# Gate modulation in the key pairs: four rounds of 512 columns in a row per pair, and rows turned by transposes

## The chip, the core and the metric

The kernel runs on one core of a Trainium2 chip. The metric is the device time of one execution in microseconds; lower is better. The engines are TensorE (PE; its weight loads are listed apart as PEld), VectorE (DVE), ScalarE (ACT), GpSimd (POOL) and SyncE (SP, which here only issues DMAs). Each has its own instruction stream; they meet only at semaphores.

## The reference

One layer of a hybrid decoder, for a prompt of 512 tokens and 8 sample sequences of 8 tokens (64), 576 token columns in all, with a model width D of 2048:

```python
mod = silu(c) @ w_ada + b_ada                     # 9 condition rows: 1 prompt, 8 samples
shift, scale, gate = split(mod, 3)                # 2048 columns each
h = rmsnorm(x, norm_pre) * (1 + scale) + shift
u = h @ w_in                                      # q, k, v, z, o, gates g_a, g_m ...
y_a = (attention(...) * silu(z_a)) @ w_br_a
y_m = (mlstm(...) * sigmoid(o) * silu(z_m)) @ w_br_m
y = (sigmoid(g_a) * y_a + sigmoid(g_m) * y_m) @ w_out
out = x + gate * rmsnorm(y, norm_post)
```

Shift and scale are needed before the first projection; gate is needed only at the very end.

## The kernel before

**Large products.** Weights come in granules of 256 KB into one of four slots of `w_raw` (SP's queue). ScalarE rounds a granule to `w_hi`, VectorE makes the remainder `w_lo` (`split_lo`), and TensorE multiplies three products: hi by hi, lo by hi, hi by lo. VectorE works three granules ahead of TensorE (`ahead`); `in_load` on SP waits on `lo_ready` until the slot's earlier granule is split, and ScalarE waits on `gemm_used` before it overwrites the slot's `w_hi`.

**First stage** (to about 187 us). 32 granules of the query columns, walked 2 row blocks at a time (`q_granule(n)`, j = n // 4, v = n % 4), because each row block of h is ready only when its shift and scale are. The shift and scale columns are made in 8 chunks: `ada_round(n)` multiplies a 1 MB piece of `w_ada` (`ada_in`, four buffers, loads of 512 KB on SP's queue, `ada_load`) by the condition rows padded to 32 columns (`c_pad`), 512 columns at a time, into `bank_a`, four matmuls side by side on four strips of the array (partitions 32t). Four rounds make a chunk. VectorE copies the bank to `mod_rows` (`ss_rows`), then `ada_rows` turns it to features: four plain fp32 matmuls with `pick`, a 128x9 matrix of ones and zeros that also sums the four strips, into 36 columns of `bank_o`; `ss_out` adds the bias in four small operations to `mod_ss`. POOL makes h from it (`s1`, `h_tmp`), ScalarE `h_hi`, VectorE `h_lo`. Between these, VectorE adds each granule's product into `q_acc` (`q_sum`), which frees the bank for the next one (`bank_free`).

**Pairs** (187 to 1134 us). Pairs of 128 columns, eight granules each: pairs 4 to 7 are the keys, 8 to 11 the attention values, and so on to 31. `k_or_v_pair` runs a key pair, with `to_tokens` (five transposes) after its first two granules for the pair before; `tok_k` on VectorE copies them and POOL stores them. In pairs 5 to 7 this is a loop (`Fori`). In pair 8 the gates of the mLSTM are summed in `bank_o` and `bank_a`. From pair 11 on, attention and mLSTM steps are laid between the granules. At 11 * NG + 4, `row_g`, `row_y` and `row_s` are turned to tokens by eleven small matmuls with the identity.

**Branch stage** (1134 to 1793 us). Four quads of 512 columns, each of 48 granules (`branch_quad(i)`, j = 0 .. 47): `ga` (16), `gm` (16), `ya` (8), `ym` (8). A granule is 12 matmuls of 512 columns and two for the samples. VectorE mixes at the end of `ya` and `ym` (`g_a`, `g_m`). Here the gate columns are made, 256 at a time in 8 chunks: after every sixth granule (j % 6 == 3) one `ada_g_round` of four matmuls of 256 columns on 9-column weights (`c_t`); the 512 KB pieces `ada_g` have one buffer and are loaded by POOL (`gate_in`), which waits on `ada_used` for each and stores and reloads `y_scratch` in between. VectorE copies four strips to `mod_row_g` at j = 22 and 46, TensorE turns them with two `pick` matmuls at j = 23 and 47, and `mod_out` adds the bias.

**Output stage** (to the end). Four quads of 16 granules with `w_out`. At kt == 9 of each, `gates_of(q)` spreads the gate over tokens with eight fp32 matmuls with the identity, four from `mod_g` broadcast and four from `g_exp`.

Of the kernel before, what the change touches and what calls it, by code (L numbers as in the profile page):

```python
# [66 lines left out]
ADA_N = ADA_CHUNKS * AQ  # L67

# [44 lines left out]
def build(nc, x_prompt, x_sample, cache_k, cache_v, state_C, state_n, state_m, page_table, c_prompt, c_sample,  # L113
# [11 lines left out]
    with ctx:  # L125
# [14 lines left out]
        def ada_slot(n):  # L140
            s = n % ADA_SLOTS
            return ada_late[s - 2] if s >= 2 and n >= ADA_N - 2 * AQ else ada_in[s]

# [34 lines left out]
        ada_late = [sb("ada_late0", "R1", 0, [P, AQ, AW]), sb("ada_late1", "R1", 4 * T, [P, AQ, AW])]  # L178
        v_att = sb("v_att", "R3", 0, [P, NT, DATT])
# [34 lines left out]
        c_t = sm("c_t", [P, KT, 9])  # L214
# [15 lines left out]
        pick = sm("pick", [P, 9])  # L230
# [107 lines left out]
        mod_row_g = sb("mod_row_g", "OT", 0, [P, CW])  # L338
        ada_g = sb("ada_g", "ROWS", 0, [P, AQ, CW])
# [29 lines left out]
        ada_g_ready = sem("ada_g_ready")  # L369
# [52 lines left out]
        def _(sp):  # L422
# [53 lines left out]
            p = 4  # L476
            for col, pairs in PH_PAIRS[1:]:
                with sp.Fori(max(p, 5), p + pairs) as i:
                    in_pair(i, sp.snap(col + (i - p) * CW))
                p += pairs  # L480
# [39 lines left out]
        def _(pe):  # L520
# [44 lines left out]
            def ada_rows(rows, n, blocks):  # L565
# [4 lines left out]
                for b in range(blocks):  # L570
                    done = mm(bank_o[:, 9 * b:9 * b + 9], rows[:, b * P:(b + 1) * P], pick[:])
# [86 lines left out]
            with pe.Fori(5, 8) as p:  # L658
                k_or_v_pair(p, 2 * (p - 5))

            for g in range(NG):
                in_granule(8, g)
                if g < 2:
                    to_tokens(stage[:, g, :], (bank_free[g], V0 + 8), (tok_done, 6 + g), tok_ps)
                if g == 4:
                    pe.wait_ge(gate_vec, 4)
# [48 lines left out]
            for x in range(11 * NG, 16 * NG):  # L715
# [14 lines left out]
                if x == 11 * NG + 4:  # L730
                    pe.wait_ge(rows_exp, 1)
                    pe.wait_ge(tok_done, 14)
                    for i in range(NT + 1):
                        n = P if i < NT else NS
                        mm(bank_s[0:n, 1, 4 * i:4 * i + 4], row_g[:, i * P:i * P + n], ident[0:HM, 0:HM])
                        mm(bank_s[0:n, 1, 32 + 4 * i:36 + 4 * i], row_y[:, i * P:i * P + n], ident[0:HM, 0:HM])
                    mm(bank_s[0:NB, 1, 64:68], row_s[:, 3 * NS:3 * NS + NB], ident[0:HM, 0:HM]).then_inc(rows_tok_ps, 1)
# [307 lines left out]
            def branch_quad(i):  # L1045
                for j in range(FGRAN):
# [14 lines left out]
            pe.wait_ge(pad_ready, 2)  # L1061
# [423 lines left out]
        def _(dve):  # L1485
# [24 lines left out]
            V.tensor_scalar(c_t[:].rearrange("p k c -> p (k c)"), c_th[:], 0.5, None, ALU.mult)  # L1510
# [14 lines left out]
            def mod_out(dst, blk, blocks, p, of):  # L1525

                dve.wait_ge(row_tp, p + 1)
                for b in range(blocks):
                    done = V.tensor_scalar(dst[:, blk + b, :], bank_o[:, 9 * b:9 * b + 9], vec_t[:, bass.ds(of + blk + b, 1)], None, ALU.add)
                done.then_inc(mod_done, 1)  # L1530
# [97 lines left out]
            for g in range(NG):  # L1628
# [22 lines left out]
                if g == 4:  # L1651
                    dve.wait_ge(gate_act, 2)
                    V.tensor_tensor(lf[:], lf2[:], lf[:], ALU.subtract).then_inc(gate_vec, 1)
            for cb in range(2):
# [10 lines left out]
            k_pair(5)  # L1665
            with dve.Fori(6, 8) as p:
# [13 lines left out]
            for g in range(NG):  # L1680
                ahead(8, g)
                if g in (1, 2):
# [261 lines left out]
            V.memset(mod_row_g[:], 0.0).then_inc(pad_ready, 1)  # L1944
# [80 lines left out]
            for x in range(S_F, S_END):  # L2025
# [17 lines left out]
                if kind == "out" and i == 0:  # L2043
                    if 3 <= kt < 7:
                        y_lo(12 + kt - 3)
                    if kt == 2:
                        mod_out(mod_g, 4 * (FQ - 1) + 2, 2, ADA_CHUNKS + 2 * FQ - 1, V_ADA + 2 * KT)
# [355 lines left out]
```

## Time and profile before

| | |
|---|---|
| median of 3 runs | 2010.16 us (2010.01 to 2010.32) |
| profiled execution, its own time | 2013.64 us |
| profiled execution, span of the profile | 2012.1 us |
| TensorE matmuls busy | 1966.6 us, 98% |
| VectorE, ScalarE, POOL busy | 784.6, 644.3, 212.5 us |
| bytes moved by DMA | 240.49 MB, mean 120 GB/s |

Busy time of TensorE counts matmuls from start to modelled end, and consecutive matmuls overlap; what a matmul adds to the time is therefore read from the starts of its neighbours. A row of the timeline gives the start, the length, engine, line, operation, destination and sources. A line such as L522 is a helper, used by all matmuls, so tiles tell the operations apart. A plain fp32 matmul leaves two records, a transpose one.

### The profile page before, as it was taken

Reading aid. Unit: us, or ns where it says so; the run is one execution under the profiler, and the core shown is the slowest. Engines: PE = TensorE matmul, PEld = TensorE weight load, DVE = VectorE, ACT = ScalarE, POOL = GpSimd, SP = SyncE. Lnnn points to the kernel's source line nnn. Section 1 sums busy time; section 2 is a strip of 40 time slices with the busy share of each in tenths; the row PEclk is TensorE's granted clock in tenths of the full one; section 3 lists DMA queues with packets and bytes.
Section 4 is the critical chain, followed back from the end, with each engine's and each line's share of the span. In section 5 each row is a group of like instructions: output and inputs, shape, how many; then the busy total and the mean of one; then the engine's idle time right before and its main releaser. Section 6 shows DMA issues by size and latency. Waiting matters only on the chain.

```text
span 2012.1 us, 31825 instructions
## 1 busy us (share of the span) xinstructions
PE 1966.6 (98%) x12466; PEld 1675.5 (83%) x12466; DVE 784.6 (39%) x1671; ACT 644.3 (32%) x1160; POOL 212.5 (11%) x351
## 2 busy tenths in 40 slices
PE   5999999999999999999999999999999999999997
PEld 4878999988899888888999877777777777778885
DVE  4555334256633234544444322422322232352224
ACT  4222222245445444432333222222212212332332
POOL 2220002000020101222410000000000000100001
PEclk9999999999999999999999999999999999999999
DMA  9983332231244532223532333343333343452223
GB/s 305 318 276 97 97 101 81 74 98 52 58 146 149 159 110 71 73 83 95 149 103 79 91 103 107 104 128 100 110 120 108 100 133 100 143 197 92 79 79 115
DMA packets 161841, 240.49 MB, mean 120 GB/s; under 512 B 15065, under 2 KB 113497, under 8 KB 159977
## 3 DMA queue, kind: packets, MB, share of 16 engines
q1 hardware_dynamic: 141600, 177.25, 29.3%
q0 software_dynamic: 17872, 61.28, 9.3%
q8 instruction: 89, 1.46, 0.3%
q10 hardware_dynamic: 2242, 0.19, 0.1%
q14 instruction: 38, 0.31, 0.0%
HBM read 220.93 MB, written 17.73 MB: 119 GB/s over the span
## 4 chain that ended last, share of the span: by engine, by line
PE 74%; DVE 1%; POOL 1%; issue 1%; ACT 1%; DMA 0%; ACTq 0%; POOLq 0%
PE gemm L522 58%; PE bank_s L522 8%; PE bank_o L522 3%; PE bank_a L522 3%; PE bank_s L754 1%; DVE g_m L1990 1%; PE bank_a L700 0%; PE bank_s L921 0%; PE bank_s L1042 0%; POOL hm_sq L2299 0%; POOL hm_sq L2300 0%; POOL rinv L2370 0%; ACT hm_sq L1124 0%; DVE y_tok L2082 0%; ACT w_hi L1124 0%
## 5 line engine op out<-in xcount | busy, mean ns | idle before, releaser
L1493 DVE TENSOR_TENSOR w_lo<-w_raw,w_hi 128x512 fp32r<-128x512 f32 x512 | 357.2, 699 | 808.0 <-ACT w_hi L1124 807.4
L522 PE MATMUL gemm<-h_hi,w_hi 128*128 128x288 f32 (+1 forms) x2560 | 666.4, 326 | 5.9 <-DVE q_acc L1563 2.4
L1124 ACT ACTIVATE w_hi<-w_raw 128x512 fp32r<-128x512 f32 x512 | 322.3, 630 | 1054.4 <-PE bank_s L522 590.7
L522 PE MATMUL gemm<-h_hi,w_lo 128*128 128x288 f32 (+1 forms) x2560 | 640.5, 316 | 0.0
L522 PE MATMUL gemm<-h_lo,w_hi 128*128 128x288 f32 (+1 forms) x2560 | 639.5, 315 | 0.0
L522 PEld LDWEIGHTS gemm<-h_hi,w_hi 128*128 128x128 f32 x2560 | 426.6, 189 | 86.2 <-issue 52.6
L522 PEld LDWEIGHTS gemm<-h_hi,w_lo 128*128 128x128 f32 x2560 | 427.3, 189 | 20.6
L522 PEld LDWEIGHTS gemm<-h_lo,w_hi 128*128 128x128 f32 x2560 | 426.9, 189 | 19.8
L522 PE MATMUL gemm<-w_hi,y_all 128*128 128x512 f32 x512 | 159.0, 392 | 0.4 <-DVE g_m L1990 0.4
L522 PEld LDWEIGHTS gemm<-w_hi,y_all 128*128 128x128 f32 x512 | 95.5, 188 | 25.2 <-DVE g_m L1990 1.1
L522 PE MATMUL gemm<-w_lo,y_all 128*128 128x512 f32 x256 | 99.9, 390 | 0.0
L2343 POOL DMA_DIRECT2D ada_g<-in_w_ada x32 | 24.1, 753 | 617.3 <-PE bank_a L522 481.5
L522 PE MATMUL gemm<-brm,w_hi 128*128 128x512 f32 x256 | 80.4, 395 | 0.0
L522 PE MATMUL gemm<-bra,w_hi 128*128 128x512 f32 x256 | 79.5, 392 | 0.0
L522 PEld LDWEIGHTS gemm<-bra,w_hi 128*128 128x128 f32 x256 | 47.8, 188 | 13.5 <-issue 1.7
L522 PEld LDWEIGHTS gemm<-brm,w_hi 128*128 128x128 f32 x256 | 47.1, 188 | 14.1 <-issue 3.4
L522 PEld LDWEIGHTS gemm<-w_lo,y_all 128*128 128x128 f32 x256 | 48.1, 188 | 10.2
L1756 DVE CUSTOM_DVE_ANT_0 e_map<-bank_s,alibi 128x128 f32<-128x128 f32 (+3 forms) x64 | 31.4, 491 | 56.9 <-PE bank_s L522 55.4
L522 PE MATMUL bank_s<-w_lo,h_smp 128*64 128x512 f32 x128 | 50.8, 397 | 0.0
L1124 ACT ACTIVATE e_map<-e_map,nmx 128x128 f32<-128x128 f32 (+3 forms) x64 | 35.5, 556 | 46.3 <-DVE nmx L1758 46.3
L522 PE MATMUL gemm<-brm,w_lo 128*128 128x512 f32 x128 | 49.9, 390 | 0.0
L522 PE MATMUL gemm<-bra,w_lo 128*128 128x512 f32 x128 | 49.9, 390 | 0.0
(454 smaller groups left out, 1794.7 us busy)
## 6 DMA issues: line engine op xcount, KB each, us to landing
w_raw<-in_w_in SPq DMA_DIRECT2D x384, 256.0 KB, 2.8
ada_in<-in_w_ada SPq DMA_DIRECT2D x56, 512.0 KB, 8.6
ada_g<-in_w_ada POOLq DMA_DIRECT2D x32, 512.0 KB, 4.3
w_raw<-in_w_out SPq DMA_DIRECT2D x64, 256.0 KB, 2.7
k_page<-in_cache_k POOLq DMA_DIRECT2D x16, 512.0 KB, 5.4
v_page<-in_cache_v POOLq DMA_DIRECT2D x16, 512.0 KB, 4.8
w_raw<-in_w_br_a SPq DMA_DIRECT2D x32, 256.0 KB, 2.7
w_raw<-in_w_br_m SPq DMA_DIRECT2D x32, 256.0 KB, 2.8
```

The costliest lines, as they stand in the source:

```text
L522: return nc.tensor.matmul(out, lhsT, rhs, start=start, stop=stop, skip_group_check=True)
L754: done = nc.tensor.transpose(bank_s[:, j // 2, (j % 2 * PAGES + pg) * P:(j % 2 * PAGES + pg + 1) * P], k_page[:, pg, h * P:(h + 1) * P], i ...
L1124: return nc.scalar.activation(out, in_, func, **kw)
L1493: V.tensor_tensor(w_lo[:, slot], w_raw[:, slot], w_hi[:, slot], ALU.subtract).then_inc(lo_ready, 1)
L1756: link(V.tensor_tensor_reduce(e_map[:, s % 2, c, 0:n], bank_s[:, c, 0:n], alibi[:, TP - n:TP], 1.0, LOW, ALU.add, ALU.max, mx[:, s % 2, c: ...
L1990: ins = V.scalar_tensor_tensor(g, g, 1.0, gemm[:, b // 2, b % 2, :], ALU.add, ALU.mult)
L2343: pool.dma_start(ada_g[:], w_ada2[r * AQ * P:(r + 1) * AQ * P, col:col + CW] .rearrange("(t p) c -> p t c", p=P)).then_inc(ada_g_ready, 16)
```

## The change

Gate columns are now made in pairs 4 to 7, 512 at a time in four chunks, by the same `ada_round` as shift and scale: after granule 6 of pair 4 + i, `gate_group(i)` runs the chunk's four rounds in a row. `ada_rows` follows after granule 0 of the next pair. The pieces are loaded by SP (`gate_load`), two DMAs of 512 KB each with whole 512-column rows, into the two `ada_in` buffers in R4 and two new ones in R3, at places in SP's order given by `GATE_LOADS`. The rounds, row copies, `mod_out` and `gate_in` of the branch stage go, as do `c_t`, `pick`, `ada_g`, `mod_row_g`. `ada_rows` uses four 128x128 transposes, so the four strips are no longer summed there: `ss_out` and `gate_out` sum them by `tensor_reduce` and then add the bias. The eleven matmuls of the row turn and the eight of `gates_of` become transposes. The loops over pairs 5 to 7 are written out.

```diff
+GATE_CHUNKS = 4
+GATE_LOADS = {NG * (5 + i) + at: (ADA_CHUNKS + 1 + i) * AQ + r for i in range(GATE_CHUNKS - 1) for r, at in enumerate((5, 6, 8, 10))}
+GATE_LOADS.update({NG * 4 + 7: ADA_N + 2, NG * 5: ADA_N + 3})
...
+        ada_gate = [ada_in[0], ada_in[1], sb("ada_gate2", "R3", 0, [P, AQ, AW]), sb("ada_gate3", "R3", AQ * AW, [P, AQ, AW])]
...
+            def gate_load(n):
+                i, r = n // AQ - ADA_CHUNKS, n % AQ
+                sp.wait_ge(ada_used, n - ADA_SLOTS + 1)
+                if n == ADA_N + 2:
+                    for cb in range(2):
+                        sp.wait_ge(bank_free[cb], V0 + 4)
+                col = 2 * D + i * AW
+                for half in range(2):
+                    row = (AQ * r + 2 * half) * P
+                    sp.dma_start(ada_slot(n)[:, 2 * half:2 * half + 2, :], w_ada2[row:row + 2 * P, col:col + AW]
+                                 .rearrange("(t p) c -> p t c", p=P)).then_inc(ada_ready[n % ADA_SLOTS], 16)
...
+                if n in (QN - 5, QN - 3):
+                    gate_load(ADA_N + (n - QN + 5) // 2)
             in_load(4, NG - 1, COL_KA)
+            gate_load(GATE_LOADS[5 * NG - 1])
...
+                    in_load(p, g, col)
+                    if NG * p + g in GATE_LOADS:
+                        gate_load(GATE_LOADS[NG * p + g])
...
                 for b in range(blocks):
-                    done = mm(bank_o[:, 9 * b:9 * b + 9], rows[:, b * P:(b + 1) * P], pick[:])
+                    done = nc.tensor.transpose(bank_o[:, b * P:(b + 1) * P], rows[:, b * P:(b + 1) * P], ident[:])
...
+            def gate_group(i):
+                for r in range(AQ):
+                    ada_round(ADA_N + AQ * i + r)
+
             def k_or_v_pair(p, n):
 
                 for g in range(NG):
                     in_granule(p, g)
+                    if g == 0 and p > 4:
+                        ada_rows(mod_rows, ADA_CHUNKS + p - 5, AQ)
+                    if g == 6:
+                        gate_group(p - 4)
...
-                        mm(bank_s[0:n, 1, 4 * i:4 * i + 4], row_g[:, i * P:i * P + n], ident[0:HM, 0:HM])
+                        nc.tensor.transpose(bank_s[0:n, 1, 4 * i:4 * i + 4], row_g[:, i * P:i * P + n], ident[0:HM, 0:HM])
...
-            def ada_g_round(i, r):
-
-                if r == 0:
-                    pe.wait_ge(row_out, ADA_CHUNKS + i)
-                pe.wait_ge(ada_g_ready, 16 * (AQ * i + r + 1))
-                for t in range(AQ):
-                    done = mm(bank_a[32 * t:32 * t + 9, 0:CW], c_t[:, AQ * r + t, :], ada_g[:, t, :], start=r == 0, stop=r == AQ - 1)
-                done.then_inc(ada_used, 1)
...
-                    if j % 6 == 3:
-                        ada_g_round(2 * i + j // 24, j // 6 % 4)
-                    if j in (23, 47):
-                        ada_rows(mod_row_g, ADA_CHUNKS + 2 * i + j // 24, 2)
...
-                    mm(bank_o[:, b * P:(b + 1) * P], mod_g[:, 4 * q + b, 0:1].to_broadcast([P, P]), ident[:])
+                    nc.tensor.transpose(bank_o[:, b * P:(b + 1) * P], mod_g[:, 4 * q + b, 0:1].to_broadcast([P, P]), ident[:])
                 for b in range(4):
-                    done = mm(bank_a[0:NS, b * P:(b + 1) * P], g_exp[:, b, :], ident[:])
+                    done = nc.tensor.transpose(bank_a[0:NS, b * P:(b + 1) * P], g_exp[:, b, :], ident[:])
...
+            def quarters(b, blocks):
+                return bank_o[:, b * P:(b + blocks) * P].rearrange("p (b t x) -> p b x t", t=AQ, x=32)[:, :, 0:9, :]
+
+            def gate_out(i):
+
+                dve.wait_ge(row_tp, ADA_CHUNKS + i + 1)
+                out = mod_g[:, AQ * i:AQ * i + AQ, :]
+                of = V_ADA + 2 * KT + AQ * i
+                link(V.tensor_reduce(out, quarters(0, AQ), AX.X, ALU.add))
+                V.tensor_tensor(out, out, bcast(vec_t[:, of:of + AQ], 9), ALU.add).then_inc(mod_done, 1)
...
-                for b in range(AQ):
-                    blk = b // 2 * KT + 2 * c + b % 2
-                    done = V.tensor_scalar(mod_ss[:, blk, :], bank_o[:, 9 * b:9 * b + 9], vec_t[:, V_ADA + blk:V_ADA + blk + 1], None, ALU.add)
+                for part in range(2):
+                    blk = part * KT + 2 * c
+                    link(V.tensor_reduce(mod_ss[:, blk:blk + 2, :], quarters(2 * part, 2), AX.X, ALU.add))
+                for part in range(2):
+                    blk = part * KT + 2 * c
+                    done = V.tensor_tensor(mod_ss[:, blk:blk + 2, :], mod_ss[:, blk:blk + 2, :], bcast(vec_t[:, V_ADA + blk:V_ADA + blk + 2], 9), ALU.add)
                 done.then_inc(mod_done, 1)
...
             def k_pair(p):
                 for g in range(NG):
                     ahead(p, g)
+                    if g == 1:
+                        gate_out(p - 5)
                     if g in (1, 2):
                         tok_k(2 * (p - 5) + g - 1)
+                ss_rows(ADA_CHUNKS + p - 4)
...
-            for n in range(2 * FQ * AQ - 2):
-                gate_in(n // AQ, n % AQ)
-                if n % (2 * AQ) == 0 and n:
-                    y_store(n // (2 * AQ) - 1)
+            for i in range(FQ - 1):
+                y_store(i)
```

## Rows read from the trace of the kernel before

**Rows 1.** Busy time by stretch: PE, PEld, DVE, ACT, POOL, PEclk, DMA share, GB/s.

```profile
40.00:172.00 132.00, 129.62 (x1000) 104.24 (x997) 68.73 (x124) 31.08 (x50) 27.57 (x56) 0.99 0.84 267
...
187.00:330.00 143.00, 143.00 (x1074) 140.71 (x1074) 52.70 (x119) 34.16 (x56) 14.80 (x19) 1.00 0.34 93
...
1134.00:1793.00 659.00, 657.57 (x3074) 511.24 (x3073) 205.72 (x346) 161.00 (x266) 36.27 (x55) 1.00 0.36 113
```

**Rows 2.** Chain of waits: start, length, what; an input pair, a branch granule.

```profile
561.53 3.19 PE gemm L522 x24
...
1197.38 2.73 PE gemm L522 x12
```

**Rows 3.** Waits of TensorE, 1120 to 1830 and 30 to 172: total, times, longest.

```profile
PEld gemm L522 <- DVE g_m L1990: 4.3, 8, 0.8
...
PE gemm L522 <- DVE q_acc L1563: 2.4, 6, 0.4
```

**Rows 4.** Timeline of TensorE around a gate round in the branch stage.

```profile
1206.57 0.40 PE L522 MATMUL bank_s<-w_lo,h_smp 128*64 128x512 f32 x1
1206.89 0.62 PE L522 MATMUL bank_a<-ada_g,c_t 128*9 128x256 f32 x8
1207.44 0.50 PE L522 MATMUL gemm<-h_hi,w_hi 128*128 128x512 f32 x1
1207.78 0.40 PE L522 MATMUL gemm<-h_lo,w_hi 128*128 128x512 f32 x1
```

**Rows 5.** Timeline of TensorE around the row turn at j = 23.

```profile
1213.71 0.40 PE L522 MATMUL bank_s<-w_lo,h_smp 128*64 128x512 f32 x1
1213.95 0.51 PE L522 MATMUL bank_o<-pick,mod_row_g 128*128 128x9 f32 x4
...
1214.62 0.39 PE L522 MATMUL gemm<-h_lo,w_hi 128*128 128x512 f32 x1
```

**Rows 6.** Timeline of TensorE around the four transposes of `fold_features`.

```profile
1193.35 0.39 PE L522 MATMUL bank_s<-w_lo,h_smp 128*64 128x512 f32 x1
1193.58 0.60 PE L1042 MATMUL bank_s<-ident,s_copy 128*128 128x128 f32 x4
...
1194.24 0.39 PE L522 MATMUL gemm<-h_lo,w_hi 128*128 128x512 f32 x1
```

**Rows 7.** Timeline of TensorE around `gates_of` (the row at 1819.22 is left out).

```profile
1816.98 0.40 PE L522 MATMUL bank_s<-w_lo,y_all 128*64 128x512 f32 x1
1817.21 1.06 PE L522 MATMUL bank_o<-ident,mod_g 128*128 128x128 f32 x8
...
1819.78 0.40 PE L522 MATMUL gemm<-w_lo,y_all 128*128 128x512 f32 x1
```

**Rows 8.** Instructions that read `row_g`: duration min/median/max, first and last start.

```profile
L522 PE MATMUL bank_s<-ident,row_g x10: 194/248/268, 393.8 to 395.8; 4*128 4x4 f32 x8, 4*64 4x4 f32 x2
```

**Rows 9.** Timeline of TensorE around the row turn in the first stage.

```profile
68.36 0.43 PE L522 MATMUL gemm<-h_hi,w_lo 128*128 128x288 f32 x2
68.64 0.95 PE L522 MATMUL bank_o<-pick,mod_rows 128*128 128x9 f32 x8
...
69.79 0.42 PE L522 MATMUL gemm<-h_lo,w_hi 128*128 128x288 f32 x2
```

**Rows 10.** VectorE: `ss_out` in the timeline, and the reductions of `lam_s`.

```profile
69.63 0.63 DVE L1546 TENSOR_SCALAR mod_ss<-bank_o,vec_t 128x9 f32<-128x9 f32 x4 [1.86 <-PE bank_o L522]
...
L1643 DVE TENSOR_REDUCE lam_s<-lam_p x2: 220/220/220, 189.0 to 189.5; 128x1 f32<-128x64 f32 x2
```

**Rows 11.** Timeline of TensorE around four rounds in the first stage.

```profile
63.01 0.43 PE L522 MATMUL gemm<-h_hi,w_lo 128*128 128x288 f32 x2
63.37 3.64 PE L522 MATMUL bank_a<-ada_in,c_pad 128*32 128x512 f32 x32
...
67.31 0.42 PE L522 MATMUL gemm<-h_lo,w_hi 128*128 128x288 f32 x2
```

**Rows 12.** DMAs into `ada_in`: time from issue to landing.

```profile
DMA to landing us min/median/max: 3.6/8.6/18.3
```

More of the change, by code:

```diff
@@ L141, in ada_slot @@
             s = n % ADA_SLOTS
+            if n >= ADA_N:
+                return ada_gate[s]
             return ada_late[s - 2] if s >= 2 and n >= ADA_N - 2 * AQ else ada_in[s]
@@ L337, in build @@
         assert work[0] == 5632
-        mod_row_g = sb("mod_row_g", "OT", 0, [P, CW])
-        ada_g = sb("ada_g", "ROWS", 0, [P, AQ, CW])
         g_exp = sb("g_exp", "OT", 0, [P, 4, NS])
@@ L474, in in_pair @@
                     in_load(p, g, col)
-            p = 4
-            for col, pairs in PH_PAIRS[1:]:
-                with sp.Fori(max(p, 5), p + pairs) as i:
+            for p, col in [(p, COL_KA + (p - 4) * CW) for p in (5, 6, 7)] + [(8, COL_VA)]:
+                for g in range(NG):
+                    in_load(p, g, col)
+                    if NG * p + g in GATE_LOADS:
+                        gate_load(GATE_LOADS[NG * p + g])
+            p = 8
+            for col, pairs in PH_PAIRS[2:]:
+                with sp.Fori(max(p, 9), p + pairs) as i:
                     in_pair(i, sp.snap(col + (i - p) * CW))
@@ L657, in _ @@
             pe.wait_ge(x_out_a, 2 * (NT + 1))
-            with pe.Fori(5, 8) as p:
+            for p in range(5, 8):
                 k_or_v_pair(p, 2 * (p - 5))
@@ L664, in _ @@
                     to_tokens(stage[:, g, :], (bank_free[g], V0 + 8), (tok_done, 6 + g), tok_ps)
+                if g == 0:
+                    ada_rows(mod_rows, ADA_CHUNKS + 3, AQ)
                 if g == 4:
+                    pe.wait_ge(mod_done, ADA_CHUNKS + GATE_CHUNKS)
                     pe.wait_ge(gate_vec, 4)
@@ L734, in _ @@
                         n = P if i < NT else NS
-                        mm(bank_s[0:n, 1, 4 * i:4 * i + 4], row_g[:, i * P:i * P + n], ident[0:HM, 0:HM])
-                        mm(bank_s[0:n, 1, 32 + 4 * i:36 + 4 * i], row_y[:, i * P:i * P + n], ident[0:HM, 0:HM])
-                    mm(bank_s[0:NB, 1, 64:68], row_s[:, 3 * NS:3 * NS + NB], ident[0:HM, 0:HM]).then_inc(rows_tok_ps, 1)
+                        nc.tensor.transpose(bank_s[0:n, 1, 4 * i:4 * i + 4], row_g[:, i * P:i * P + n], ident[0:HM, 0:HM])
+                        nc.tensor.transpose(bank_s[0:n, 1, 32 + 4 * i:36 + 4 * i], row_y[:, i * P:i * P + n], ident[0:HM, 0:HM])
+                    nc.tensor.transpose(bank_s[0:NB, 1, 64:68], row_s[:, 3 * NS:3 * NS + NB], ident[0:HM, 0:HM]).then_inc(rows_tok_ps, 1)
                     pe.wait_ge(rows_tok, 1)
@@ L1523, in row_copy @@
                 V.tensor_copy(dst, src).then_inc(row_out, 1)
[L1525 to L1530, printed above, removed]
+            def quarters(b, blocks):
[6 more added lines that the diff above has]
+                V.tensor_tensor(out, out, bcast(vec_t[:, of:of + AQ], 9), ALU.add).then_inc(mod_done, 1)
             def x_out(tt):
@@ L1659, in k_pair @@
                     ahead(p, g)
+                    if g == 1:
+                        gate_out(p - 5)
                     if g in (1, 2):
                         tok_k(2 * (p - 5) + g - 1)
+                ss_rows(ADA_CHUNKS + p - 4)
                 for cb in range(2):
                     keep(p, cb, 2 * (p - 4) + cb)
-            k_pair(5)
-            with dve.Fori(6, 8) as p:
+            for p in range(5, 8):
                 k_pair(p)
@@ L1681, in _ @@
                 ahead(8, g)
+                if g == 1:
+                    gate_out(3)
                 if g in (1, 2):
@@ L2046, in _ @@
                     if kt == 2:
-                        mod_out(mod_g, 4 * (FQ - 1) + 2, 2, ADA_CHUNKS + 2 * FQ - 1, V_ADA + 2 * KT)
-                        dve.wait_ge(mod_done, ADA_CHUNKS + 8)
+                        dve.wait_ge(mod_done, ADA_CHUNKS + GATE_CHUNKS)
                         link(V.tensor_tensor(mod_g[:], mod_g[:], bcast(vec_t[:, V_POST:V_POST + KT], 9), ALU.mult))
@@ L2056, in _ @@
                     mix(kind, m)
-                if x < S_G:
-                    j = x - S_F - FGRAN * i
-                    if j in (22, 46):
-                        dve.wait_ge(ada_used, ADA_N + AQ * (2 * i + j // 24 + 1))
-                        for t in range(AQ):
-                            done = V.tensor_copy(mod_row_g[32 * t:32 * t + 9, :], bank_a[32 * t:32 * t + 9, 0:CW])
-                        done.then_inc(row_out, 1)
-                    if j == 26:
-                        mod_out(mod_g, 4 * i, 2, ADA_CHUNKS + 2 * i, V_ADA + 2 * KT)
-                    if j == 2 and i:
-                        mod_out(mod_g, 4 * i - 2, 2, ADA_CHUNKS + 2 * i - 1, V_ADA + 2 * KT)
                 if kind == "out" and kt == n - 1 and i < FQ - 1:
@@ L2119, in _ @@
                                  pattern=[[1, P]], channel_multiplier=-1))
-            for t in range(AQ):
-                link(G.affine_select(out=pick[:], in_=pick[:], compare_op=ALU.not_equal, fill=1.0, base=-32 * t,
-                                     pattern=[[-1, 9]], channel_multiplier=1))
             link(G.memset(g_pick[:], 0.0))
@@ L2335, in _ @@
                 pool.dma_start(n_sample[0, :, hd, :], n_out[:]).then_inc(n_outs, 16)
[L2338 to L2344 removed]
             pool.wait_ge(c_outs[1], 64 * HM)
[L2347 to L2350 removed]
+            for i in range(FQ - 1):
+                y_store(i)
             pool.wait_ge(y_stored, 64 * (FQ - 1))
             pool.wait_ge(gemm_used, S_F + FGRAN * (FQ - 1) + 2 * KT)
[L2353 to L2359 removed]
+            for blk in range(12):
                 y_load(blk)
```

22 lines of the change are left out of this document (1 added, 21 removed).

## The prediction, made before the changed kernel was run

> **What bounds the kernel now.** I read the stretches first. In all three shown, TensorE is busy for nearly the whole stretch at a granted clock of 0.99 to 1.00 (2.4 GHz), while VectorE, ScalarE and the DMA engines have room [rows 1]. The chain of waits says the same in detail: it is made of matmuls back to back, 24 of 288 columns in 3.19 us (0.266 us a pair) in the input pairs, and 12 of 512 columns in 2.73 us (0.2275 us each) in the branch stage [rows 2]. So whatever TensorE executes inside a stretch lengthens it by its own start-to-start time, and whatever is taken out gives that time back. The waits show the few places where this is not so: in the branch stage TensorE waits 4.3 us for VectorE's `g_m` (the mixing at the end of `ym`, eight times), and in the first stage 2.4 us, six times, for `q_acc` [rows 3]. Work removed just before such a wait gives nothing.
>
> **What is removed from the branch stage.** There are 32 `ada_g_round` calls (4 quads times `j % 6 == 3`, 8 each). Around one, the last ordinary matmul starts at 1206.57 and the second ordinary one after the round at 1207.78: 1.21 us, of which two ordinary steps are 0.455, so a round costs 0.755 [rows 4]. 32 x 0.755 = 24.2 us. At the borders ga to gm and ya to ym a round stands before a new bank; I count these in full, because no wait for ScalarE is recorded at gm to ya, which has no round there either.
>
> The eight `ada_rows(mod_row_g, ..)` calls: from 1213.71 to 1214.62, again two ordinary steps plus the call, 0.91 - 0.455 = 0.455 [rows 5]. Four of them (j = 23) give it back: 1.8 us. The four at j = 47 stand right before the wait for `g_m`, which VectorE ends by its own order; TensorE will come 0.455 earlier and wait 0.455 longer. I put these at nothing. Bounds for the eight: 1.8 to 3.6. VectorE's 32 row copies and its `mod_out` work, and POOL's 32 loads and their waits, go too; neither is on the path.
>
> **What becomes a transpose.** `fold_features` does four 128x128 transposes: from 1193.35 to 1194.24, 0.89 - 0.455 = 0.435 us, 0.11 each [rows 6]. `gates_of` does eight fp32 matmuls of 128 columns: from 1816.98 to 1819.78 with three ordinary steps, 2.80 - 0.68 = 2.12 us, 0.265 each [rows 7]. As transposes 8 x 0.11 = 0.87, so 1.25 saved, four times: 5.0 us. The Trainium skill ("TensorE: Matmul & The Clock Gate", section Terms) calls the transpose mode four times faster for fp32; by that, `gates_of` would take 0.53 and the four calls would give 6.4. Rows 6 and 7 show 2.4 times, and the sum goes by them.
>
> The turn of `row_g` and `row_y`: five of each and one of `row_s` in turn, in two passes each, starting from 393.8 to 395.8 [rows 8], with the last one some 2.2 us. Eleven at 0.11 are 1.2, so 1.0 is saved. The wait for `rows_tok` behind it stays. Bounds: 0.5 (if tiny transposes have an issue cost of their own) to 1.5.
>
> **The first stage.** The eight `ada_rows` there have four matmuls: from 68.36 to 69.79, 1.43 - 0.53 = 0.90 us [rows 9]; as transposes 0.435, so 0.465 less on TensorE. But right behind it VectorE runs `ss_out`, a `w_lo` and the `q_acc` sum that frees the bank for which TensorE then waits. `ss_out` is four operations in 0.63 us now [rows 10] and becomes two reductions of 72 elements, each waited for, and two additions. The nearest row is a reduction of 64 elements at 220 ns [rows 10]; two of them start at 189.0 and 189.5 with a multiplication of 64 elements between, each waited for, so 0.26 for each waited operation at most. 2 x 0.26, and 0.37 for the two additions (an estimate: 0.16 for each of the four operations now, a little more for 18 elements): 0.89, which is 0.26 more. VectorE starts 0.35 to 0.45 earlier and runs 0.26 longer: six chunks give 0.1 each rather than 0.465. The chunk without `q_acc` sums gives 0.47 in full; the first `ss_out`, which starts late because of the three `w_lo` before it, costs 0.26 before the first matmul. Sum 0.8 us saved. Bounds: reductions twice as dear (+0.44 each call) lose 6 x 0.34 + 0.7 - 0.5 = 2.2; all transposes given back gives 3.3.
>
> **What is added to pairs 4 to 7.** `gate_group(i)` is four `ada_round` calls in a row, 16 matmuls of 512 columns on 32-column weights, four side by side. The first stage has just this group: from 63.01 to 67.31, 4.30 - 0.53 = 3.77 us, 0.94 a round [rows 11]. A round of 512 columns thus costs 0.94 against 2 x 0.755 for the two of 256 that it replaces. 4 x 3.77 = 15.1 us. Four `ada_rows` of four transposes at 0.435: 1.7 us. Both lie on the path, since TensorE is 143.00 of 143.00 us busy there [rows 1]. VectorE gets per pair one row copy (0.7 us) and one `gate_out` (0.5), in a stretch in which it is busy 52.7 of 143 us and works three granules ahead, some 9 us: hidden. Behind `gate_out` stand `tok_k` and the next `w_lo`; both have more than a granule.
>
> **The moved loads.** 16.8 MB go from POOL's queue to SP's, 32 DMAs of 512 KB. SP sends the `w_raw` load of a granule when the split of the granule four earlier is done, some seven granules ahead of TensorE; ScalarE can use it once TensorE is three granules ahead, so a load has four granules less the split, some 11 us, of cover. `gate_load` waits for a used slot: for group i+1 the first two are let go by the rounds of group i itself, the last is queued behind the `w_raw` load of granule 10 (the next pair's third), which goes when TensorE has ended the pair's granule 2 and the split has followed, 1.3 us later. Its round comes after granule 6 and three rounds: 4 x 3.19 + 2.8 - 1.3 = 14.3 us. A 512 KB load in the crowded first stage landed in 8.6 us at the median and 18.3 at the longest [rows 12], where the core moved 267 GB/s. In the pairs it moves 93 [rows 1], and 16.8 MB over some 120 us add 140: 233 GB/s, below what the first stage reached. I cost the wait at nothing. The first group has even more time (its last two loads wait for the `q_acc` tiles in R3 to be read, six granules before use). `h_hi` and `h_lo` tiles are no longer touched. Without this cover each late microsecond counts once per pair.
>
> **The sum.** Saved: 24.2 + 1.8 + 5.0 + 1.0 + 0.8 = 32.8. Added: 15.1 + 1.7 = 16.8. Net 16.0 us less. The profiled execution spans 2012.1 us (2013.6 with what lies around it), 3.5 above the median of the runs; I take the difference as unchanged: span 1996.1, median 2010.2 - 16.0 = 1994.2.
>
> **The rivals.**
> *The groups wait for their loads (slower).* Place: TensorE before the fourth round of groups 1 to 3, SP's queue behind it. Up to a landing time of 14.3 us nothing happens; at 18.3, the longest seen, three waits of 4.0, 12 us: 2006. It decides the sign when three waits take 16.0, that is at 19.6 us; at 23 they take 26 and the time is about 2020. For it: 512 KB loads and 256 KB `w_raw` loads share one queue, and a blocked SP holds back both. Against: the measured rate has room. 5 in 100 for slower, 7 in 100 for a partial wait (1997 to 2006).
> *VectorE decides the first stage.* `ss_out` with dear reductions, and the h chain (POOL, ScalarE, VectorE) behind it late by the same: 2 to 5 us lost, 1997 to 2001. For it: six waits for `q_acc` now. 12 in 100.
> *More comes back than I count.* Faster transposes, the j = 47 calls counted, the first stage giving all: 1.8 + 2.5 + 1.4 + 0.5, at most 6: 1988 to 1991. 10 in 100.
> *The branch rounds were no cost.* If the removed rounds filled time in which TensorE had to wait for the split weights, the time would rise by 15.1 + 1.7 - 6.8 = 10 us, 2020. Against it, ScalarE is busy 161 and VectorE 206 of the 659 us there [rows 1]. 1 in 100.
> *The clock falls behind runs of transposes.* There are 17 places with new ones; a granule of 3.19 us at 1.2 GHz behind each would cost 54 us, 2048. The input pairs already hold `to_tokens` transposes twice a pair and run at 1.00 [rows 1]. 2 in 100. The Trainium skill (the same page, Part 4) says that transposes do not count as TensorE being busy in the way that matmuls do; by that rule this case would be real only if a run of them were long, and here it is below 1 us.
> *My sum:* 63 in 100, 1991 to 1997.
>
> **Range and chances.** From 1989.5 to 2002.0: it leaves out the slow rivals (8 in 100), half of the partial wait and some of the gains. Faster by over 0.2% (4 us, about what a measurement of this kernel can tell from no change): all cases that end below 2006, 0.91. Within it 0.03, slower 0.06.
>
> **What would show each step.** In the profile after: no matmul of `ada_g`, and branch granules one after the other; stretch 1134 to 1793 shorter by 26 us. Groups of 16 matmuls in pairs 4 to 7, each 3.6 to 3.8 us with no idle time before it; if TensorE shows waits for DMAs of `ada_in` or `ada_gate` there, the first rival is true. `gates_of` 0.9 us. VectorE's `mod_ss` group 0.8 to 1.0 us, and TensorE's wait for `q_acc` near 0.4 us as before; above 0.7 us the second rival. TensorE's wait for `g_m` grows by about 1.8 us. The pairs 4 to 8 become 16.8 us longer. The prediction is wrong if the groups cost well over 3.8 us, for which a wait or a lower clock must be seen.

## The result, and the profile after

| | before | after |
|---|---|---|
| median | 2010.09 us (2009.66 to 2010.32) | 1992.62 us (1992.08 to 1994.67) |
| profiled execution: span of the profile | 2012.1 us | 1990.6 us |
| TensorE matmuls busy | 1966.6 us | 1940.9 us |

The ratio is 0.991, with a 95% interval of 0.9898 to 0.9923: 17.5 us less, where 16.0 had been forecast. Both kernels were run once more: after 1992.65 us against 2010.71 for before beside it, and before unchanged 2010.65 against 2011.21. The medians of before, in all sets of executions, run from 2010.1 to 2011.2 us, so a median moves by some 0.5 to 1 us. Single executions moved by up to 2.6 us for the kernel after (4 and 4 executions) and by up to 6.4 for before (2009.24 to 2015.6 among 15).

The stretches of the profile after, with the columns of [rows 1]:

```profile
40.00:172.00 132.00, 127.01 (x980) 101.12 (x972) 70.19 (x125) 31.06 (x50) 27.66 (x56) 0.99 0.84 267
187.00:330.00 143.00, 143.00 (x1090) 129.56 (x1091) 42.74 (x89) 29.95 (x49) 10.67 (x16) 1.00 0.59 189
1134.00:1793.00 659.00, 656.73 (x2932) 528.98 (x2931) 201.77 (x321) 169.42 (x279) 15.58 (x29) 1.00 0.31 98
```

In the pairs TensorE is still busy for all of 143.00 us, with DMA traffic twice that of [rows 1] (189 against 93 GB/s). Now the waits of TensorE that answer to [rows 3], the whole execution's list (total, times, longest):

```profile
PEld gemm L543 <- DVE g_m L2018: 5.6, 8, 0.8
...
PE gemm L543 <- DVE q_acc L1587: 4.0, 6, 0.7
...
PE gemm L543 <- DVE g_m L2018: 2.2, 8, 0.4
...
PE bank_o L947 <- DMA n<-in_state_n: 1.6, 1, 1.6
```

For 187 to 330 us the same view lists no wait of TensorE at all: the groups of rounds never waited for a load. The wait for `g_m` grew from 4.3 to 5.6 on the weight loads, and from 1.4 to 2.2 on the matmuls. These are two views of the same pauses (two at the end of each quad), so they are not added; the 4.3 of [rows 3] is the weight loads' figure. The wait for `q_acc` grew from 2.4 to 4.0.

The timeline of the kernel after at a group of rounds in pair 4, at the row turn (rows 410.11 to 410.55, alike, left out), at `gates_of`, and at `ss_out` in the first stage:

```profile
209.34 0.42 PE L543 MATMUL gemm<-h_hi,w_lo 128*128 128x288 f32 x2
209.70 1.93 PE L543 MATMUL bank_a<-ada_in,c_pad 128*32 128x512 f32 x16
211.44 1.90 PE L543 MATMUL bank_a<-ada_gate,c_pad 128*32 128x512 f32 x16
213.27 0.53 PE L543 MATMUL gemm<-h_hi,w_hi 128*128 128x288 f32 x2
213.64 0.42 PE L543 MATMUL gemm<-h_lo,w_hi 128*128 128x288 f32 x2
...
410.03 0.22 PE L767 MATMUL bank_s<-ident,row_g 4*128 4x4 f32 x1
...
410.61 0.16 PE L769 MATMUL bank_s<-ident,row_s 4*8 4x4 f32 x1
411.31 0.53 PE L543 MATMUL gemm<-h_hi,w_hi 128*128 128x288 f32 x2 [0.54 <-DVE dec_tok L1772]
...
1800.43 0.40 PE L543 MATMUL bank_s<-w_lo,y_all 128*64 128x512 f32 x1
1800.66 0.60 PE L1089 MATMUL bank_o<-ident,mod_g 128*128 128x128 f32 x4
1801.10 0.60 PE L1091 MATMUL bank_a<-ident,g_exp 128*64 128x128 f32 x4
...
1802.01 0.39 PE L543 MATMUL gemm<-w_lo,y_all 128*128 128x512 f32 x1
...
87.87 0.60 PE L592 MATMUL bank_o<-ident,mod_rows 128*128 128x128 f32 x4
...
88.51 0.50 DVE L1567 TENSOR_REDUCE mod_ss<-bank_o 128x18 f32<-128x72 f32 x2 [1.50 <-PE bank_o L592]
...
89.04 0.27 DVE L1570 TENSOR_TENSOR mod_ss<-mod_ss,vec_t 128x18 f32<-128x18 f32 x2
...
90.72 0.50 PE L543 MATMUL gemm<-h_hi,w_hi 128*128 128x288 f32 x2 [0.66 <-DVE q_acc L1587]
```

A group is 16 + 16 records, with no idle time before any of them. From 209.34 to 213.64, less two ordinary steps (0.53), it takes 3.77 us, just what [rows 11] gave. The row turn starts at 410.03 and its eleventh transpose at 410.61: 0.6 us, where [rows 8] had some 2.2. `gates_of` is 1802.01 - 1800.43 less three ordinary steps (0.68): 0.90 us, where [rows 7] had 2.12. `ss_out` is two reductions in 0.50 and two additions in 0.27.

**Where the time went.** Starts of the same instructions, read from the tile views, cut the span into parts. The two right columns use the second profile of before and of after; the first profile of before lay above its median, and the part in bold is why.

| part of the span, us | before | after | before again | after again | forecast change |
|---|---|---|---|---|---|
| start to the row turn | 393.8 | 410.0 | 393.2 | 409.0 | +16.0 |
| row turn to the first `exp` of `e_map` | 9.4 | 6.2 | 9.3 | 6.2 | -1.0 |
| first `z_act` to the head step's `c_a` transposes | **135.1** | 132.3 | 132.3 | 133.9 | 0 |
| last `z_act` to the last `s_copy` (branch stage) | 657.9 | 631.3 | 658.0 | 631.3 | -26.0 |
| last `s_copy` to the end | 220.5 | 215.5 | 220.5 | 215.5 | -5.0 |

The parts not shown are the same to 0.2 us. Between the second profiles the span falls from 2008.6 to 1991.3: 15.8 - 3.1 + 1.6 - 26.7 - 5.0 = -17.4. Three rows are as forecast to within 0.7 us; the row turn gives three times its term; and the part in bold, which the change does not touch, differs from one execution to the next. So does the first part, by up to 1.0 us between two profiles of one kernel (410.0 and 409.0).

### The profile page after: what moved, and what is told of

Same layout as the page of the kernel before. It is cut to its first block, busy times and chain, and to the rows that moved or that the text cites. A ratio compares the mean times of both kernels' runs of the same rounds, so it can differ in the third digit from the quotient of the medians.

```text
span 1990.6 us, 31173 instructions
## 1 busy us (share of the span) xinstructions
PE 1940.9 (98%) x12247; PEld 1661.4 (83%) x12247; DVE 773.6 (39%) x1633; ACT 644.4 (32%) x1160; POOL 187.7 (9%) x314
## 4 chain that ended last, share of the span: by engine, by line
PE 74%; DVE 1%; POOL 1%; issue 1%; ACT 1%; DMA 0%; ACTq 0%; POOLq 0%
PE gemm L543 58%; PE bank_s L543 9%; PE bank_o L543 3%; PE bank_a L543 2%; PE bank_s L786 1%; DVE g_m L2018 1%; PE bank_a L732 0%; PE bank_s L953 0%; PE bank_s L1065 0%; POOL hm_sq L2311 0%; POOL hm_sq L2312 0%; POOL rinv L2366 0%; ACT hm_sq L1142 0%; DVE y_tok L2098 0%; PE bank_s L572 0%
## 5 line engine op out<-in xcount | busy, mean ns | idle before, releaser
L543 PEld LDWEIGHTS gemm<-h_hi,w_lo 128*128 128x128 f32 x2560 | 425.4, 188 | 20.3
L2292 POOL DMA_DIRECT2D y_scratch<-g_a x12 | 6.5, 546 | 574.9 <-DVE g_a L2037 574.1
```

What stands on the lines that cost most here:

```text
L543: return nc.tensor.matmul(out, lhsT, rhs, start=start, stop=stop, skip_group_check=True)
L2292: pool.dma_start(y_scratch[4 * i + b], g_a[:, b, :]).then_inc(y_stored, 16)
```

## The experiments

**The first two: both kernels again.** The kernels after and before, unchanged, beside others.

> The changed kernel unaltered, beside the others on one chip. My sum: 16 us below the kernel before. The theory that the granted clock adds to it (it stood at 0.68 for 5 us behind the row turn and at 0.50 for 5 us behind the head-3 mLSTM step in the profile before, and at 1.00 in both places in the one after): 17 to 18 us below, because the fall behind the row turn is gone in every run (1.4 us), while the fall behind the head-3 step comes and goes and spreads single times over some 3 us.

Measured: 1992.65 us (1991.78 to 1993.91), ratio 0.9909 (0.9894 to 0.9924). It is 18.1 below the 2010.71 beside it, nearer to the 17 to 18 of the clock theory than to the 16 of the sum, but the first set gave 17.5, so the medians alone hardly decide between the two.

The later experiments are given against this 1992.65, though some were run in other sets. The kernel before had 2010.71 in this set (with the row turn by matmuls, the transposes alone, and after without gate work), 2010.56 beside rounds apart, late loads, `pick` and the small vector first, and 2010.27 beside the last three; differences across sets are uncertain by about as much.

> The kernel before, unaltered, for a second profile of it. The first was taken of an execution 3.5 us above the median. From the start of the row turn to the first attention exponential it took 9.4 us there (9.3 in e1, 6.2 wherever the turn is made of transposes), and from the first z_act to the sample states' transposes 135.1 us (132.2 to 133.9 in the others). If the fall of the clock behind the row turn belongs to the matmul turn, the first interval is again 9.3 to 9.4, and the second, which comes and goes, is 132 to 134. If both come and go, the first can be near 7.8.

Measured: 2010.65 us, ratio 0.9997 (0.9988 to 1.0006), span 2008.6 us. The earlier profiled execution of before, at 2012.1, was thus no picture of its median: the bold 135.1 above is 132.3 in this one.

**The row turn by matmuls in the kernel after.**

```diff
-  nc.tensor.transpose(bank_s[0:n, 1, 4 * i:4 * i + 4], row_g[..], ident[0:HM, 0:HM])
+  mm(bank_s[0:n, 1, 4 * i:4 * i + 4], row_g[..], ident[0:HM, 0:HM])
   (the same for row_y and row_s)
```

> The changed kernel with the eleven transposes of the row turn put back to matmuls with the identity. My sum's term: 1.0 us more than e0; by the start times of the two profiles 1.6 (2.2 us against 0.6). If the clock theory holds, the turn takes 1.6 us more and the granule behind it shows a granted clock well below 1.00 again, which costs another 1.4: 3.0 more in all.

Measured: 1995.25 us, ratio 0.9923 (0.9909 to 0.9936): 2.6 above the kernel after beside it, where the term was 1.0. Windows around the turn tell why; the columns are those of [rows 1], and the granted clock is the third number from the end. First this kernel:

```profile
409.30:412.20 2.90, 2.36 (x24) 2.22 (x23) 0.51 (x6) 0.63 (x1) 0.00 (x0) 1.00 0.24 82
412.20:417.50 5.30, 5.30 (x29) 4.90 (x29) 0.96 (x2) 0.28 (x1) 1.90 (x4) 0.68 0.19 49
```

The kernel before, and before again:

```profile
396.70:402.00 5.30, 5.24 (x28) 4.88 (x28) 1.03 (x3) 0.28 (x1) 1.89 (x4) 0.68 0.18 49
```

```profile
397.00:402.00 5.00, 5.00 (x28) 4.72 (x27) 0.75 (x4) 0.63 (x1) 1.15 (x3) 0.68 0.18 52
```

The kernel after:

```profile
410.00:411.30 1.30, 0.77 (x12) 0.64 (x11) 0.49 (x6) 0.63 (x1) 0.00 (x0) 1.00 0.50 165
411.30:415.00 3.70, 3.69 (x28) 3.52 (x28) 0.99 (x2) 0.14 (x1) 1.90 (x4) 1.00 0.27 71
```

With matmuls, the 5 us behind the turn ran at a mean granted clock of 0.68, between the two levels of 2.4 and 1.2 GHz. With transposes they ran at 1.00, and the same 28 or 29 matmul records took 3.7 us in place of 5.3. So the turn gives twice: 1.6 us of its own, and about 1.5 of clock behind it. The interval from the turn to `e_map` was 9.3 to 9.4 us in all four profiles with the matmul turn (before twice, this one, and the kernel before without gate work) and 6.1 to 6.2 in the ten others.

**The transposes alone, in the kernel before** (row turn and `gates_of`; the first stage as it was).

> The kernel before with only the row turn and the eight matmuls of each gates_of made transposes; nothing moved. My sum: 5.0 + 1.0 = 6.0 us below before. With the clock theory 5.0 + 1.6 + 1.4 = 8.0 below. The rule that a transpose is four times faster than an fp32 matmul would give 6.4 + 1.6 = 8.0 without any change of clock; the start times in gates_of tell the two apart (0.9 us for eight, or 0.5).

Measured: 2004.56 us, ratio 0.9967 (0.9954 to 0.9981), 6.15 less than before. By its profile against before again: -3.1 at the turn, -5.0 in the output stage, but the part shown in bold was 133.8 and not 132.3, 1.5 more, and 0.6 more to the row turn; span 2002.7 against 2008.6. The median thus lies at the 6.0 of the sum and not at the 8.0 of the clock theory; the profile has the whole 8.1 of the two changed places and loses 2.1 elsewhere. The experiment on the head step below shows what the 1.5 of it is.

**The kernel after without gate work.**

```diff
-  if g == 6:
-      gate_group(p - 4)
   (and the gate row turns, row copies, gate_out, gate_load and their waits)
+  V.memset(mod_g[:], 1.0)
```

> The changed kernel without the gate part of the modulation: no gate loads, rounds, row copies, row transposes and gate_out; mod_g is filled with ones. My sum: 16.8 us below e0 (four groups of 3.77, four row turns of 0.43), with no other difference. If the added loads or VectorE work cost TensorE anything beyond their own matmuls, the gap is above 18; if part of the groups is hidden somewhere, it is below 15.

Measured: 1976.06 us, ratio 0.9824 (0.9809 to 0.9839): 16.6 below the kernel after. The added work costs what the sum said, 16.8, to within 0.2 by the medians and 0.4 by the profiles (the row turn starts at 392.6 in place of 409.0): next to nothing of it is hidden, and next to nothing is lost around it.

**The kernel before without gate work.**

```diff
-  if j % 6 == 3:
-      ada_g_round(2 * i + j // 24, j // 6 % 4)
-  if j in (23, 47):
-      ada_rows(mod_row_g, ADA_CHUNKS + 2 * i + j // 24, 2)
   (and the row copies, mod_out and gate_in)
+  V.memset(mod_g[:], 1.0)
```

> The kernel before without the gate part of the modulation: no rounds, row turns, copies and loads in the branch stage; mod_g is filled with ones. My sum for what the branch stage gives back: 26.0 us below before (32 rounds at 0.755, four row turns, four more hidden behind the wait for g_m). If rounds at the borders of products had been hidden, eight of 32, the gap is near 20; if all row turns count, 27.8. The two profiles give 26.6 for the stretch.

Measured: 1984.0 us, ratio 0.987 (0.9852 to 0.9887): 26.3 below before, 26.0 forecast. Its branch stage is 631.3 us, as in the kernel after.

**The rounds apart, one after each of granules 3 to 6 of the pair.**

```diff
-  if g == 6:
-      gate_group(p - 4)
+  if g >= 3 and g < 7:
+      ada_round(ADA_N + AQ * (p - 4) + g - 3)
```

> The changed kernel with the four rounds of a gate chunk laid apart, one after each of granules 3 to 6 of the pair instead of all after granule 6. If a run of four saves only the columns, no change. By the rows: a lone round of 256 columns cost 0.755, a round of 512 in a run of four 0.94; if a lone round has a fixed part for getting in and out of the four-strip matmuls (0.4 us if the column part of 256 is half of 0.85), a lone one of 512 costs about 1.15 to 1.2, so 16 x 0.2 to 0.25 = 3 to 4 us more than the changed kernel.

Measured: 1997.48 us, ratio 0.9933 (0.9919 to 0.9946), 4.8 above the kernel after. The timeline of a lone round:

```profile
231.33 0.42 PE L543 MATMUL gemm<-h_hi,w_lo 128*128 128x288 f32 x2
231.68 1.06 PE L543 MATMUL bank_a<-ada_in,c_pad 128*32 128x512 f32 x8
232.68 0.53 PE L543 MATMUL gemm<-h_hi,w_hi 128*128 128x288 f32 x2
233.04 0.42 PE L543 MATMUL gemm<-h_lo,w_hi 128*128 128x288 f32 x2
```

From 231.33 to 233.04 less two ordinary steps (0.53) is 1.18 us, against 0.94 in a run of four. Sixteen rounds at 0.24 more are 3.8 us; the period of a pair, from one `mod_rows` copy to the next, is 31.7 us in place of 30.9, which is 3.4 in all. That is most of the 4.8; the rest was not placed. A round costs its border as well as its columns, so putting four in a row is a part of the gain in its own right.

**The gate loads late in SP's order.**

```diff
-  for r, at in enumerate((5, 6, 8, 10))
+  for r, at in enumerate((7, 8, 10, 14))
```

> The changed kernel with the loads of groups 1 to 3 sent later: at positions 7, 8, 10, 14 of SP's order instead of 5, 6, 8, 10. The last piece then goes about 1.5 us before its round can start, instead of 14.3. In the profile after, pieces landed in 5.5 us (4.3 to 6.7). First rival's mechanism: three waits of 4 to 5 us each, 12 to 15 us more than the changed kernel, and TensorE's waits name the DMA into ada_gate. If the group hides the wait, or the clock falls behind it, the sum differs: a fall of the clock adds up to 3 us each.

Measured: 2013.95 us, ratio 1.0018 (1.0009 to 1.0027), 21.3 above the kernel after. The list of waits and the timeline at one of them:

```profile
PE bank_a L543 <- DMA ada_gate<-in_w_ada: 14.7, 3, 5.0
```

```profile
242.08 1.04 PE L543 MATMUL bank_a<-ada_gate,c_pad 128*32 128x512 f32 x8
247.99 1.93 PE L543 MATMUL bank_a<-ada_gate,c_pad 128*32 128x512 f32 x8 [4.87 <-DMA ada_gate<-in_w_ada]
249.85 0.85 PE L543 MATMUL gemm<-h_hi,w_hi 128*128 128x288 f32 x2
250.50 0.68 PE L543 MATMUL gemm<-h_lo,w_hi 128*128 128x288 f32 x2
250.98 0.68 PE L543 MATMUL gemm<-h_hi,w_lo 128*128 128x288 f32 x2
...
252.26 0.42 PE L543 MATMUL gemm<-h_hi,w_lo 128*128 128x288 f32 x2
```

The wait itself is 4.9 us, yet it costs about 6.9: the round behind it takes 1.86 us from start to start in place of 0.94, and the next pairs start 0.48 apart in place of 0.27, which is TensorE at 1.2 GHz until about 252. From one group to the next it is 37.8 and 37.7 us where the kernel after has 30.9, so the first two waits cost 6.9 and 6.8; from the third group to the row turn it is 6.6 more. Together that is 20.3, and the row turn starts 20 to 21 us later. The waits alone, 14.7, are what the first rival's mechanism was expected to give (12 to 15); the rest is what comes behind them. The first rival was a real danger: with loads sent two to four granules later in SP's order the whole gain is gone. In the kernel after the slack held, but it was smaller than the prediction's 14.3 us. Its last group has the last load issued and the third of its rounds started so:

```profile
293.43 0.99 SPq L449 DMA_DIRECT2D ada_gate<-in_w_ada  x2
```

```profile
304.02 1.90 PE L543 MATMUL bank_a<-ada_gate,c_pad 128*32 128x512 f32 x16
```

The second DMA is issued at 293.94 and the fourth round starts at 304.88: 10.9 us. In the two groups before it is 12.0 and 11.4. `ada_gate` landed in 5.5 us at the median and 6.7 at the longest, so some 4 us were left, not 8.

**The strips summed by `pick` again,** in the first stage and for the four gate turns; `ss_out` and `gate_out` four additions each, as before.

```diff
-  done = nc.tensor.transpose(bank_o[:, b * P:(b + 1) * P], rows[:, b * P:(b + 1) * P], ident[:])
+  done = mm(bank_o[:, 9 * b:9 * b + 9], rows[:, b * P:(b + 1) * P], pick[:])
```

> The changed kernel with the twelve row turns put back to fp32 matmuls with pick, and with the four small additions in place of reductions. My sum: 0.8 us back in the first stage, and four turns in the pairs at 0.90 instead of 0.43: 1.9. Together 2.7 us more than the changed kernel. The theory that VectorE eats the first stage's saving entirely: 1.9 us more or less than that; the theory that transposes pay in full: 12 x 0.465 = 5.6 more.

Measured: 1995.83 us, ratio 0.9923 (0.9909 to 0.9936), 3.2 above the kernel after, 2.7 forecast. Four gate turns at 0.465 are 1.9 of it, which leaves 1.3 for the first stage, for which the sum had 0.8. In the first stage of the kernel after, a chunk takes 18.71 us from one `mod_rows` copy to the next, and took 18.89 before: 0.18 saved, where the prediction had 0.1. Six such are 1.1.

**The sum that frees a bank first, then `ss_out`.** VectorE's order in the first stage, at v == 1:

```diff
-  if v == 1 and more:
-      ss_out(c + 1)
   early_lo(n + LOOKAHEAD)
-  if c:
-      q_sum(c, v, n)
+  if v == 1 and more:
+      if c:
+          q_sum(c, v, n, (0,))
+      ss_out(c + 1)
+      if c:
+          q_sum(c, v, n, (1,))
+  elif c:
+      q_sum(c, v, n)
```

> The changed kernel with one order changed on VectorE in the first stage: at v == 1 the split of the next granule and the q_acc sum of the first bank go before ss_out, not behind it. In the profile after, TensorE waits 0.66 us for that sum in six chunks, while VectorE stands idle 1.5 us before each ss_out. If this wait is what eats the saving of the row transposes there, it goes and the time falls by 4.0 us (6 x 0.66). If the later ss_out then holds up h (about 0.2 us later, with some 1 us of room), less: 1 to 3 us, with waits for h_lo or h_tmp in its place.

Measured: 1988.67 us, ratio 0.989 (0.9872 to 0.9907), 4.0 below the kernel after (3.5 if each is taken against before in its own set), as expected. A chunk takes 17.82 us, 0.89 less and not the 0.66 of the wait; this holds for five intervals, 4.5 us, and the interval before them is about 1 us longer (19.1, against 17.7 and 18.4 in the two profiles of the kernel after). So there is luck in how well the 4.0 came out. The list of waits of 30 to 180 us has no wait of TensorE for VectorE's `q_acc` any more, and instead:

```profile
PEld gemm L543 <- DVE h_lo L1576: 1.0, 1, 1.0
...
PE bank_s L543 <- POOL h_tmp L2198: 0.8, 1, 0.8
...
PE gemm L543 <- ACT q_acc L1142: 0.6, 1, 0.6
```

These are short and come once each; the h chain mostly has room for an `ss_out` that comes a little later. So the kernel after was held in each of six chunks by `ss_out` standing ahead of the `q_acc` sum: the place that the prediction's second rival named, though it cost a few us by the order of VectorE's work and not through a dear reduction. The kernel before has the same order and waits for `q_acc` six times too [rows 3]; the edit was not tried there.

**The small state vector loaded before the large state.** At the last mLSTM head TensorE waits 1.6 us for `n` (the fourth row of the waits above), whose DMA stands behind the four loads of the large state on POOL's queue.

```diff
+  pool.dma_start(n0[:], state_n[0]).then_inc(in_n0, 16)
   state_in(0, 0)
-  pool.dma_start(n0[:], state_n[0]).then_inc(in_n0, 16)
```

> The changed kernel with one order changed on POOL: the small load of the sample states n goes before the four loads of the states C, not behind them (2.9 us of issuing). In the profiles before and after TensorE waits 1.6 us for it, at the end of 6 us in which it is busy 4.5, and behind this the clock stood at 0.50 once and at 1.00 once. Wait alone: 1.6 us less. If the stretch is also what lets the clock fall, the single times also lie closer together and the median falls by 2 to 3 us.

Measured: 1990.39 us, ratio 0.9899 (0.9884 to 0.9915), 2.3 below the kernel after. The wait is gone from the list (its 1.6 us is most of the 2.3), and the part in bold of the table is 130.7 us here and 130.6 in the next kernel. In the others it was 132.1 to 132.3 in four profiles, 133.7 to 133.9 in seven and 135.1 in one. The windows of this place, at the same distance behind the first `z_act` to 0.1 us, in the first profile of before:

```profile
890.00:895.00 5.00, 4.67 (x19) 4.65 (x20) 4.26 (x15) 0.35 (x1) 0.81 (x2) 0.50 0.12 33
895.00:900.00 5.00, 5.00 (x34) 5.00 (x34) 0.76 (x2) 0.63 (x1) 0.00 (x0) 0.83 0.31 79
```

in before again:

```profile
889.20:894.20 5.00, 4.67 (x35) 4.66 (x36) 4.31 (x16) 0.98 (x2) 0.95 (x2) 1.00 0.13 33
```

and in the two profiles of the kernel after:

```profile
903.00:908.00 5.00, 4.71 (x35) 4.69 (x36) 4.34 (x16) 0.98 (x2) 0.87 (x2) 1.00 0.12 34
```

```profile
901.90:906.90 5.00, 4.61 (x23) 4.59 (x24) 4.25 (x15) 0.35 (x1) 0.87 (x2) 0.66 0.11 31
```

One and the same kernel ran this stretch at 0.50 in one execution and at 1.00 in another: 19 matmul records in 5 us against 35. Over the 10 us from the start of these windows the mean granted clock is 1.00 in the four profiles with 132.1 to 132.3, 0.83 in the seven with 133.7 to 133.9, 0.67 in the one with 135.1, and 1.00 in the two without the wait. So the clock goes with the whole spread of this part, 1.6 or 2.8 us. It is not all that executions of one kernel differ by. The expectation that single times would lie closer together without this wait was not met: they run from 1989.26 to 1991.83, 2.6 us, as much as those of the kernel after. Those of before run over 6.4.

**Both edits together.**

> Both reorderings on the changed kernel: the q_acc sum before ss_out, and the load of the sample states n before that of the states C. They lie in different stretches, so their gains should add: e7 took 2.3 us off, e9 is expected to take 4.0, together 6.3, some 1986.4 us.

Measured: 1986.49 us (1985.5 to 1986.92), ratio 0.9879 (0.9861 to 0.9897): 6.2 below the kernel after (5.7 if each is taken against before in its own set) and 24 below before, the sum of the two. It is the fastest version found.

## Why the prediction held, and where its sum was off

The time, 1992.6, lies in the range, and in the interval given for the likeliest case (1991 to 1997). By its steps:

- *Branch stage, 26.0 saved:* 26.6 to 26.7 in the profiles, 26.3 with the gate work alone taken out. The turns at j = 47 gave nothing, as argued: at the end of the first quad it takes 4.71 us from the first `g_m` operation of VectorE (1293.45) to the matmul that waits longest for it in the kernel before, and 4.70 (from 1296.89) in the kernel after, with a turn on TensorE in between in the one and none in the other. The 0.6 more than forecast was not placed.
- *`gates_of`, 5.0:* the output stage is 5.0 shorter, and one call takes 0.90 us (0.87 forecast). By the four times of the Trainium skill ("TensorE: Matmul & The Clock Gate", Terms) a call would have been 0.53, an estimate; the trace shows 2.12 against 0.90 us, 2.4 times, and does not agree.
- *Groups and their row turns, 16.8 added:* 16.6 when taken out. The loads were hidden, with no wait recorded in the pairs; the experiment with late loads shows that this was the step on which the sign hung. The prediction's slack of 14.3 us was too large: the trace has 10.9 to 12.0. The core moved 189 GB/s and not the 233 added up. The outcome was right, with a margin half as wide as was worked out.
- *First stage, 0.8 saved:* the `ss_out` estimate of 0.89 us was close (0.50 and 0.27, start to end 0.80), but TensorE's wait for `q_acc` behind it still grew from 0.4 to 0.7 us at its longest. 1.3 by the `pick` experiment, 0.6 to 1.2 by the profiles, in which the start itself moves by up to 1.0; so 0.8 is neither confirmed nor refuted closely.
- *Row turn, 1.0 saved:* **this term was mis-sized.** The turn alone gives 1.6, since a transpose of four rows takes 0.06 us and not the 0.11 of a 128-row one, and the clock behind it 1.5 more: 3.1 in every profile. The prediction had the 2.2 us of the matmuls from [rows 8], but 1.2 and not 0.6 for the transposes, and no clock; the window behind the turn (0.68) was not part of its working, as [rows 1] covers other stretches. By medians the turn is worth 2.6 (undone in the kernel after) or 1.2 (done in the kernel before, less 5.0 for `gates_of`); these differ by about the spread that the bold part brings.
- *The profiled execution's excess of 3.5 us taken as unchanged:* it was not. It was the bold part, 2.8 us longer in that one profile, and 0.7 before the row turn. The sum was made on changes alone and so took no harm.
- *The clock rival:* no fall of the clock was seen behind the new transposes; the one fall in the first stage, at 36 to 43 us, stands in both kernels, and begins within a wait of 4.5 to 5.5 us for `h_tmp` that ends at 39 us. The Trainium skill (same page, Part 4) says that transposes do not count as TensorE being busy in the same way. The trace does not test that: replacing matmuls by transposes removed a fall here, but it also made the stretch shorter, 1.3 us to the next granule in place of 2.9, and no run parts the two.

Together, second profiles against each other: -0.2 at the start, -2.1 at the turn, +1.6 in the bold part, -0.7 in the branch stage, 0.0 at the end, -1.4 of the 1.5 that were missed. What stays open is whether the fall in the bold part comes more often when the earlier one is gone: in seven of the eight profiles with the transposed turn and the old order of `n0` it was 133.7 or more, but in only one of the four with the matmul turn. That is suggestive and no more.

## What to carry to other kernels

Where TensorE is busy end to end, start-to-start times of its own neighbours priced added and removed work to within a few per cent (16.8 and 26.0 against 16.6 and 26.3). A group cost 3.77 us in the first stage and in the pairs alike, while a turn right before a wait gave nothing. Borders count too: four rounds in a row cost 0.94 us each, alone 1.18. Look at the granted clock in the microseconds behind every short pause of TensorE, not only over whole stages: what shortens it can give as much again in clock, as at the row turn (1.6 and 1.5). When work is moved to a queue, work out the slack of each load from its place in the order, and read it from the trace afterwards, since a wait of 4.9 us there cost 6.6 to 6.9.

## What had not been expected of the hardware

- Eleven tiny matmuls and the wait behind them, 2.9 us with TensorE busy 2.4, were followed by 5 us at a granted clock of 0.66 to 0.68 in four profiles of four; the same work as transposes, 1.3 us to the next granule, by 1.00 in ten of ten.
- A pause of 1.6 us with a thin stretch around it (TensorE busy 4.5 to 4.6 of the 6 us before) was followed by 0.50 in one execution and 1.00 in another of the same kernel; the fall is not fixed by the program alone.
- 512 KB loads landed in 5.5 us at the median in the pairs (4.3 to 6.7) at 189 GB/s, against 8.6 in the first stage [rows 12] at 267 GB/s.
